# State-space matrices of a Hymba block on one core: turned by VectorE instead of TensorE, and the kernel blocks made in one visit

## The chip, the cores and the metric

The kernel runs on one core of one Trainium2 chip. The metric is the device time of one execution in microseconds, the median of three runs. The engines are TensorE (PE), VectorE (DVE), ScalarE (ACT), GpSimd (POOL) and SyncE (SP), which here only issues DMAs. Each engine runs its own instructions in order and waits on semaphores for the others.

## The reference

One block over x of 1 x 1024 x 1024 (1024 positions, width 1024), float32:

```
x = x + 1/2 * SwiGLU_1(RMSNorm(x))                 # 1024 -> 2816 -> 1024
h = RMSNorm(x); [q | k | v | u] = h @ w_in
attn = banded_sink_attention(q, k, v, sink)         # window 2 chunks of 64
ssm  = s5_ssm_glu(u, ...)
x = x + concat(RMSNorm(attn), RMSNorm(ssm)) @ w_out
x = x + 1/2 * SwiGLU_2(RMSNorm(x));  return RMSNorm(x)
```

The change lies in the state-space part: 32 groups g of 16 channels h, with 64 complex states p each:

```
lam_bar = exp(lam * exp(log_dt));  b_bar = ((lam_bar - 1) / lam) * b
s_t = lam_bar * s_(t-1) + b_bar u_t                 # associative scan over 1024 positions
y   = Re(c s) + d_skip * u;  z = gelu(y);  ssm = z * sigmoid(z @ w_glu + b_glu)
```

## The kernel before

**Products.** Every large product is made of fp32r parts: each factor is split into a high and a low part, and `mm3` (L1185 to L1187) issues three 128x128x512 matmuls, high by low, low by high and high by high. ACT makes the high parts (L1800, L1884), DVE the low ones (L2405, L2570, L2575).

**Order of the whole.** The first SwiGLU comes first, as 22 instances of seven products each (Strassen's scheme on gate and up, instances n = 0 to 21, `instance(n)` on each engine, 19.0 us each), then the down projection in 77 steps q (`down`, 12 matmuls, 2.72 us each). Then RMSNorm, the input projection, the mixer (state space and attention), the output projection, and the second SwiGLU like the first. In `down`, DVE works up to four steps ahead of PE: at step q it makes the parts of step q + 4 (`down_w`, `down_b`), and it adds weights (L2596) and takes results.

**State-space matrices.** They depend only on parameters, and POOL makes them beside the first SwiGLU, in one long chain of small operations in which each waits for the one before:
- It loads a_re, a_im and log_dt into `par` (`params`; L3107 issues log_dt, paced by the count of products that PE has done, `products(n, s)`), waits for them, and loads b (L3113, `load_b`) and c (L3118, `load_c`) at places of its chain where it works out the powers `lam` of lam_bar and `Bb`, that is b_bar.
- c comes as (g h) x p and is needed as p x (g h). PE transposes it at instance 10 (`c_tiles`, eight transposes), and ACT copies it to `CT` (`c_out`). POOL makes `CL`, c times the powers, from it.
- In a loop of four passes (from L3330, i = 0 to 3; four of the sixteen pairs j of groups each) POOL makes `EBb`, b_bar times the powers, to be E once turned, stores it to `eb_scratch` (L3356), waits for the store, since it writes the same buffer again (L3359), and makes and stores `cs`, the powers of the eighth power.
- Behind the loop, POOL adds squares for the sum of squares of the mixer's norm (L3071). They are issued in order, so they can't start before the loop has ended. PE reads the sum in `norm_sum` (L1211).

**Visits.** During the input projection PE leaves its large products for short visits. `WITH_PE` names them: at (unit, half) it lists the steps, each issued behind that unit's product. `WITH_ACT` and `MIXER_DVE` are ACT's and DVE's own lists. The steps are:
- E0 to E7 (`transposes_e`, L1485): four transposes each of `ebs`, which SP loaded from `eb_scratch`. ACT copies the results to `Et` (`e_out`). Two visits of four steps.
- K0 to K3 (`blocks_k`, L1479): the blocks of the convolution kernel, `Bb` times `CL`, 16 written matmuls of 64x16 by 64x128 a step, into partitions 0 to 15 of two banks. For g2 = 0 and 1 they use partitions 0 to 63 and 64 to 127 as input rows. ACT (`k_out`) and DVE (`k_first`, which adds d_skip on the diagonal, `dgl`) copy them to `kst`, and SP stores them to `k_scratch`. One visit each.
- I0 to I3 (`inject`, L1505): `Et` times `u8`, what u puts into the states. DVE takes it and scans.
- Y0 to Y3 (`outputs_y`, L1527, L1534): `Mt` times u8 plus `CL` times the states. `Mt` is read back from `k_scratch` (`load_m`).

Steps use banks 4 to 7 in turn (`ROUND`, `round_free`), so each waits for what was read four rounds before.

**SP's queue.** SP issues all of these loads and stores in one order, written out by hand (L1101 to L1145): behind the last product of the down projection x is stored and `ebs` and `CL` are loaded, then `load_in` (weights of the input projection), `store_u` and `load_u8` (u through memory into `u8`, L1046), `load_csn` (the powers cs), `store_k`, `load_m`, the bias, `store_y`. An issue of SP that waits holds back all that stand behind it.

Of the kernel before, what the change touches and what calls it, by code (L numbers as in the profile page):

```python
# [122 lines left out]
def taken_in(o):  # L123
# [30 lines left out]

ROUND = [((kind, 2 * b + i) if kind == "K" else (kind, b), 0 if kind == "K" else i)
         for kind, b in sum((WITH_PE[o] for o in sorted(WITH_PE)), []) if kind in "KEIY"
         for i in range(1 if kind == "E" else 2)]
# [242 lines left out]
CONST_DMAS = 4 + 2 + 1 + 8 + 1  # L400
# [23 lines left out]
def block_kernel(nc, x, ff1_norm, ff1_w_gate, ff1_w_up, ff1_w_down, mix_norm, w_in, sink, a_re, a_im,  # L424
# [85 lines left out]
    ebs = at("ebs", 64 * KB, [P, 2, NJ, P])  # L510
    csn = [at(f"csn{b}", (64 + 4 * b) * KB, [P, 2, 4, NC]) for b in range(4)]
# [3 lines left out]
    kst = [at(f"kst{i}", (80 + 4 * i) * KB, [GH, 8, P]) for i in range(2)]  # L515
# [3 lines left out]
    Et = at("Et", 162 * KB, [P, NJ, 2, P])  # L519
    Mt = at("Mt", 162 * KB, [P, NG, P])  # L520
    qT = at("qT", 162 * KB, [P, L // CHUNK, GQ, CHUNK])
    dgl = at("dgl", 178 * KB, [GH, NG, GH])
# [26 lines left out]
    dsk = small("dsk", [GH, NG])  # L549
# [99 lines left out]
    eb_d = nc.dram_tensor("eb_scratch", (P, 2, NJ, P), F32, kind="Internal").ap()  # L649
# [72 lines left out]
    ct_ready = sem("ct_ready")  # L722
# [2769 lines left out]
```

## Time and profile before

| | us |
|---|---|
| median of three runs | 1590.37 (1590.2 to 1590.79) |
| the profiled execution's own time | 1590.72 |
| its span | 1588.9 |
| PE busy | 1580.6 (99%) |
| DVE busy | 1096.8 (69%) |
| ACT busy | 714.3 (45%) |
| POOL busy | 512.5 (32%) |

The span is the time from the first to the last recorded instruction; the profiled execution took 1590.72 - 1588.9 = 1.8 us more, around it. Matmuls are pipelined: a record shows about 0.39 us for a large one, while the next starts 0.227 us behind it, so what PE spends is read from start to start. Busy time alone says little about the engines beside PE; what counts is whether PE has to wait for them.

### The profile page before, as it was taken

The numbers are of one execution on the slowest core, as the hardware profiler recorded it, in microseconds if no ns is written. First come the engines' busy times: TensorE is split into PE (matmuls) and PEld (weight loads), VectorE is DVE, ScalarE is ACT, GpSimd is POOL, SyncE is SP. The second block draws the span as 40 slices with busy tenths as digits, with TensorE's granted clock in tenths as the row PEclk, the third lists the DMA queues.
The fourth block names the chain that finished last, engine by engine and source line by source line (L and its number), as shares of the span: only waits on it lengthen the run. The fifth ranks groups of instructions, "written<-read, shape, count | busy, mean of one in ns | idle before, by whom it ended". The sixth has DMA issues, their size and how long they took to land.

```text
span 1588.9 us, 22029 instructions
## 1 busy us (share of the span) xinstructions
PE 1580.6 (99%) x7537; PEld 1305.3 (82%) x7537; DVE 1096.8 (69%) x1731; ACT 714.3 (45%) x1323; POOL 512.5 (32%) x938
## 2 busy tenths in 40 slices
PE   9999999999999999999999999999999999999998
PEld 7888888888888888888887888888888888888887
DVE  7966667766569886854369768766566666578766
ACT  7544343433334444532567544434344343344444
POOL 3005788877768778323030250000000000000000
PEclk9999999999999999999999999999999999999999
DMA  8253334433488545766631131433333333885443
GB/s 287 92 80 111 119 119 148 146 138 124 166 318 265 139 137 135 271 182 151 133 133 41 54 134 53 131 106 106 106 107 106 106 106 129 309 279 152 123 110 139
DMA packets 158455, 230.06 MB, mean 145 GB/s; under 512 B 25864, under 2 KB 95120, under 8 KB 154768
## 3 DMA queue, kind: packets, MB, share of 16 engines
q1 hardware_dynamic: 155120, 221.02, 43.6%
q0 software_dynamic: 3072, 7.62, 2.6%
q8 instruction: 61, 1.00, 0.3%
q14 instruction: 42, 0.34, 0.1%
q10 hardware_dynamic: 160, 0.07, 0.0%
HBM read 153.47 MB, written 74.15 MB: 143 GB/s over the span
## 4 chain that ended last, share of the span: by engine, by line
PE 98%; POOL 1%; ACT 0%; DMA 0%; DVE 0%; issue 0%; SPq 0%; DVEq 0%; POOLq 0%; ACTq 0%
PE bank L1185 31%; PE bank L1186 31%; PE bank L1187 31%; POOL ssq L3071 1%; PE bank L1552 1%; PE bank L1579 1%; PE bank L1534 0%; PE bank L1505 0%; PE bank L1479 0%; PE bank L1565 0%; PE bank L1527 0%; DMA x_in<-in_x_dram 0%; PE bank L1714 0%; PE bank L1219 0%; PE bank L1412 0%
## 5 line engine op out<-in xcount | busy, mean ns | idle before, releaser
L1185 PE MATMUL bank<-hbhi,ws_lo 128*128 128x512 f32 x1040 | 405.2, 390 | 0.0
L1187 PE MATMUL bank<-hbhi,ws_hi 128*128 128x512 f32 x1040 | 404.7, 389 | 0.0
L1186 PE MATMUL bank<-hblo,ws_hi 128*128 128x512 f32 x1040 | 404.6, 389 | 0.0
L1187 PEld LDWEIGHTS bank<-hbhi,ws_hi 128*128 128x128 f32 x1040 | 195.2, 188 | 40.7
L1185 PEld LDWEIGHTS bank<-hbhi,ws_lo 128*128 128x128 f32 x1040 | 195.2, 188 | 40.6 <-issue 0.4
L1186 PEld LDWEIGHTS bank<-hblo,ws_hi 128*128 128x128 f32 x1040 | 195.3, 188 | 40.3
L3071 POOL TENSOR_TENSOR ssq<-ssq,sqt 128x512 f32<-128x512 f32 x18 | 25.2, 1401 | 615.1 <-ACT sqt L1767 613.4
L1185 PE MATMUL bank<-d_hi,ws_lo 128*128 128x512 f32 x572 | 222.8, 389 | 0.0
L1187 PE MATMUL bank<-d_hi,ws_hi 128*128 128x512 f32 x572 | 222.5, 389 | 0.0
L1186 PE MATMUL bank<-d_lo,ws_hi 128*128 128x512 f32 x572 | 222.5, 389 | 0.0
L1837 ACT ACTIVATE loc<-bank 128x512 f32<-128x512 f32 x160 | 95.6, 597 | 251.6 <-PE bank L1187 251.6
L1884 ACT ACTIVATE d_hi<-d_in 128x512 fp32r<-128x512 f32 x154 | 96.0, 628 | 199.9 <-DMA d_in<-b_scratch 199.6
L2405 DVE TENSOR_TENSOR ws_lo<-w_sum,ws_hi 128x512 fp32r<-128x512 f32 x160 | 115.1, 719 | 97.3 <-ACT ws_hi L1800 97.3
L2575 DVE TENSOR_TENSOR d_lo<-d_in,d_hi 128x512 fp32r<-128x512 f32 x154 | 113.7, 740 | 82.9 <-ACT d_hi L1884 82.7
L1800 ACT ACTIVATE ws_hi<-w_sum 128x512 fp32r<-128x512 f32 x160 | 100.2, 626 | 76.2 <-PE bank L1187 60.1
L1185 PEld LDWEIGHTS bank<-d_hi,ws_lo 128*128 128x128 f32 x572 | 107.4, 188 | 22.7 <-issue 0.4
L1187 PEld LDWEIGHTS bank<-d_hi,ws_hi 128*128 128x128 f32 x572 | 107.4, 188 | 22.4
L1186 PEld LDWEIGHTS bank<-d_lo,ws_hi 128*128 128x128 f32 x572 | 107.4, 188 | 21.9
L1185 PE MATMUL bank<-hT_hi,w_lo 128*128 128x512 f32 x288 | 116.0, 403 | 0.0
L1186 PE MATMUL bank<-hT_lo,w_hi 128*128 128x512 f32 x288 | 112.4, 390 | 0.0
L1187 PE MATMUL bank<-hT_hi,w_hi 128*128 128x512 f32 x288 | 112.4, 390 | 0.0
L2405 DVE TENSOR_TENSOR ws_lo<-raw2a,ws_hi 128x512 fp32r<-128x512 f32 x78 | 55.0, 712 | 64.5 <-ACT ws_hi L1800 63.7
(319 smaller groups left out, 2696.6 us busy)
## 6 DMA issues: line engine op xcount, KB each, us to landing
b_scratch<-loc SPq DMA_DIRECT2D x42, 1024.0 KB, 7.3
d_in<-b_scratch SPq DMA_DIRECT2D x154, 256.0 KB, 3.1
raw2a<-in_ff_w_up_dram SPq DMA_DIRECT2D x42, 512.0 KB, 4.9
loc<-in_ff_w_gate_dram SPq DMA_DIRECT2D x36, 512.0 KB, 4.9
xT<-x_scratch SPq DMA_DIRECT2D x12, 1024.0 KB, 6.6
x_scratch<-xT SPq DMA_DIRECT2D x5, 2048.0 KB, 8.2
dw_lo_place<-in_ff_w_down_dram SPq DMA_DIRECT2D x8, 1024.0 KB, 7.9
x_in<-in_x_dram SPq DMA_DIRECT2D x8, 512.0 KB, 7.7
```

The source lines that it names most:

```text
L1185: nc.tensor.matmul(o, wl, rh, start=first, stop=False, skip_group_check=chain)
L1186: nc.tensor.matmul(o, wh, rl, start=False, stop=False, skip_group_check=chain)
L1187: return nc.tensor.matmul(o, wh, rh, start=False, stop=last, skip_group_check=chain)
L1552: last = nc.tensor.matmul(o, qT[r, n, 2 * a:2 * a + 2, :].rearrange("p g q -> p (g q)"), kTp[r, n * CHUNK:n * CHUNK + P], start=True, stop ...
L1579: last = nc.tensor.matmul(bank[V_BANK[m]][kv * HD:(kv + 1) * HD, nn * 256:(nn + 1) * 256], vwin[:, 2 * m + nn, kv * HD:(kv + 1) * HD], pts ...
L1800: act.activation(as_block(ws_hi[b][:, :]), weights(n, s), ACT.Copy).then_inc(ws_hi_done, 1)
L1837: act.activation(snap[w][:, i, :], bank[inst_bank(n, role)][:, :], ACT.Copy).then_inc(snap_taken, 1)
L1884: act.activation(d_hi[q % N_SLOT][:, :], d_in[q % N_SLOT][:, :], ACT.Copy).then_inc(d_hi_done, 1)
L2405: dve.tensor_tensor(as_block(ws_lo[b][:, :]), weights(n, s), as_block(ws_hi[b][:, :].bitcast(F32)), ALU.subtract).then_inc(ws_lo_done, 1)
L2575: dve.tensor_tensor(d_lo[q % N_SLOT][:, :], d_in[q % N_SLOT][:, :], d_hi[q % N_SLOT][:, :].bitcast(F32), ALU.subtract).then_inc(d_lo_done, 1)
L3071: pool.tensor_tensor(ssq_of(norm, h), ssq_of(norm, h), sqt_of(norm, a), ALU.add).then_inc(ssq_done, 1)
```

## The change

- `c_tiles` and `c_out` are gone. c is loaded in 16 pieces, laid out so that a transpose within blocks of 32 x 32 gives `CT`, and DVE does this in `turn_c` (two instructions) at instance 8. The loads move ahead in POOL's chain.
- `transposes_e`, `e_out` and `ebs` are gone. In each pass of POOL's loop DVE turns `EBb` to `EBt` (`turn_e`, two instructions, in blocks of 32 x 32), at instances 16 and 20 and at steps 21 and 52 of the down projection. POOL waits for the turn and stores `EBt` with four DMAs, in pieces of 128 bytes, into `et_scratch`; SP loads `Et` from there with four DMAs. POOL no longer waits for the store itself within a pass.
- `blocks_k` is one visit of 64 written matmuls behind unit 6, half 0. Its outputs lie at partitions 0, 32, 64 and 96 of two banks. `k_out` and `k_first` are two each instead of eight, the diagonal is laid out for 128 partitions, and `store_k` issues four DMAs for each of two g2; `load_m` waits for all eight.
- I3 comes behind Y0 in the same visit, at (10, 0) instead of (9, 1).
- a_re, a_im and log_dt are issued at earlier products: log_dt's last at the fourth product of instance 3 instead of instance 4. d_skip is loaded with eight DMAs instead of one.
- On SP's queue csn(0) and csn(1) come before load_in(4), and store_k(1) stands beside store_k(0).
- Buffers move: `Et`, `Mt` and the four `csn` change places, and POOL's loop has a temporary of its own.

The diff, cut to its core (removed lines are left out where the function stands above as it was):

```diff
-WITH_PE = {(1, 1): steps("m1"), (4, 0): steps("E0 E1 E2 E3"), (5, 0): steps("E4 E5 E6 E7"), (6, 0): steps("K0"), (6, 1): steps("I0"),
-           (7, 0): steps("I1 K1"), (7, 1): steps("I2"), (8, 0): steps("K2"), (8, 1): steps("K3"), (9, 1): steps("I3"),
-           (10, 0): steps("Y0"), (10, 1): steps("Y1"), (11, 1): steps("Y2"), (12, 0): steps("Y3")}
-
-WITH_ACT = {3: steps("e0 e1 e2 e3 W3"), 4: steps("e4 e5 e6 e7 W4"), 5: steps("k0 k1 W5"), 6: steps("k2 k3"),
-            7: steps("W6 k4 k5 k6 k7"), 9: steps("y0 W7"), 10: steps("y1"), 11: steps("y2 W8"),
+WITH_PE = {(1, 1): steps("m1"), (6, 0): steps("K0"), (6, 1): steps("I0"),
+           (7, 0): steps("I1"), (7, 1): steps("I2"),
+           (10, 0): steps("Y0 I3"), (10, 1): steps("Y1"), (11, 1): steps("Y2"), (12, 0): steps("Y3")}
+
+WITH_ACT = {3: steps("W3"), 4: steps("W4"), 5: steps("k0 k1 W5"),
+            7: steps("W6"), 9: steps("y0 W7"), 10: steps("y1"), 11: steps("y2 W8"),
             12: steps("y3 g0 g1"), 13: steps("W9 g2"), 14: steps("g3"), 15: steps("W10")}
-MIXER_DVE = steps("W3 D0 W4 d0 d1 W5 R0 R1 d2 d3 R2 W6 d4 d5 d6 d7 R3 b3 W7 v0 v1 W8 z0 z1 W9 z2 z3 W10")
+MIXER_DVE = steps("W3 D0 W4 d0 d1 W5 R0 R1 R2 W6 R3 b3 W7 v0 v1 W8 z0 z1 W9 z2 z3 W10")
...
+E_TURN_INST = {16: (0, 0), 20: (1, 2)}
+E_TURN_STEP = {21: 2, 52: 3}
+E_STORES = 4 + 1
+
+
...
-CONST_DMAS = 4 + 2 + 1 + 8 + 1
+CONST_DMAS = 4 + 2 + 1 + 8 + 8
 def src_of(tile, permuted):
...
-    ebs = at("ebs", 64 * KB, [P, 2, NJ, P])
-    kst = [at(f"kst{i}", (80 + 4 * i) * KB, [GH, 8, P]) for i in range(2)]
+    kst = at("kst", 80 * KB, [P, 2, 4, P])
-    Et = at("Et", 162 * KB, [P, NJ, 2, P])
+    Et = at("Et", 64 * KB, [P, NJ, 2, P])
+    EBt = at("EBt", a_v + 6 * KB, [P, 4, 2, P])
-    eb_d = nc.dram_tensor("eb_scratch", (P, 2, NJ, P), F32, kind="Internal").ap()
+    et_d = nc.dram_tensor("et_scratch", (32, NJ, 2, 4, P), F32, kind="Internal").ap()
...
         def load_csn(b):
-            sp.wait_ge(e_ready, 4 if b == 0 else 8)
             if b:
                 sp.wait_ge(cs_loaded, 16 * b)
+            if b == 2:
+                wait_lo(sp, 2 * KD)
             sp.dma_start(csn[b][:, :, :, :], cs_d[:, :, 4 * b:4 * b + 4, :]).then_inc(cs_loaded, 16)
         k_v = k_d.rearrange("g h c -> h g c")
-        def store_k(p):
-            sp.wait_ge(k_taken, 2 * p + 2)
-            if p:
-                sp.wait_ge(k_stored, 16 * p)
-            sp.dma_start(k_v[:, 8 * p:8 * p + 8, (T - 1) * GH:], kst[p % 2][:, :, :]).then_inc(k_stored, 16)
+        def store_k(g2):
+            sp.wait_ge(k_taken, g2 + 1)
+            for jj in range(4):
+                sp.dma_start(k_v[:, 2 * jj + g2::8, (T - 1) * GH:], kst[32 * jj:32 * jj + GH, g2, :, :]
+                             ).then_inc(k_stored, 16)
         def load_m(b):
             if b == 0:
                 sp.wait_ge(zero_stored, 48)
             if b >= 2:
                 sp.wait_ge(m_loaded[b % 2], 16 * T)
-            sp.wait_ge(k_stored, 16 * (b + 1))
+            sp.wait_ge(k_stored, 16 * 8)
...
-        sp.wait_ge(eb_stored, 4 * 32 + 16)
-        sp.dma_start(ebs[:, :, :, :], eb_d).then_inc(eb_loaded, 16)
+        sp.wait_ge(eb_stored, 4 * E_STORES * 16 + 16)
+        for b in range(P // 32):
+            sp.dma_start(Et[32 * b:32 * b + 32, :, :, :], et_d[:, :, :, b, :]).then_inc(et_loaded, 16)
         for i in range(2):
             sp.wait_ge(cl_stored[i], 16 * (NJ // 2))
         sp.dma_start(CL[:, :, :, :], cl_d).then_inc(cl_loaded, 16)
         load_in(3)
         sp.wait_ge(down_taken, 32)
         sp.dma_start(xs_d[:, 0:4, hs(1)], xT[:, 0:4, hs(1)]).then_inc(x_parked, 16)
+        load_csn(0)
+        load_csn(1)
         load_in(4)
         store_u(0)
-        load_csn(0)
         load_u8(0)
         load_in(5)
         store_u(1)
-        load_csn(1)
         load_u8(1)
         store_u(2)
         load_csn(2)
         load_u8(2)
         load_csn(3)
         store_k(0)
+        store_k(1)
         load_in(6)
         load_m(0)
-        store_k(1)
         store_u(3)
         load_in(7)
         load_u8(3)
         load_m(1)
-        store_k(2)
         load_m(2)
         load_glu(0)
-        store_k(3)
-        sp.wait_ge(k_stored, 64)
         sp.dma_start(biast[:, :, :], bias_c).then_inc(bias_loaded, 16)
         load_m(3)
...
+        def blocks_k(_):
+
+            pe.wait_ge(cl_loaded, 16)
             for g2 in range(2):
...
+                round_free("K", g2)
+            for p in range(4):
                 for ri in range(2):
...
+                    for jj in range(4):
+                        for g2 in range(2):
+                            r = slice(g2 * NS, (g2 + 1) * NS)
+                            last = nc.tensor.matmul(bank[round_bank("K", g2)][32 * jj:32 * jj + GH, p * P:(p + 1) * P],
+                                                    Bb[r, ri, 4 * p + jj, :], CL[r, ri, 4 * p + jj, 0:P],
+                                                    start=ri == 0, stop=ri == 1, skip_group_check=True)
+                            if p == jj == 3 and ri:
+                                last.then_inc(k_ready, 1)
         def inject(b):
-            pe.wait_ge(e_taken, 2 * b + 2)
+            pe.wait_ge(et_loaded, 64)
...
+        def k_out(g2):
+
+            act.wait_ge(k_ready, g2 + 1)
+            src = bank[round_bank("K", g2)][:, :].rearrange("q (p m) -> q p m", p=4)[:, :, GH:]
+            act.activation(kst[:, g2, :, GH:], src, ACT.Copy).then_inc(k_act, 1)
...
             for q in range(6 * N_PAIR):
                 p, j = divmod(q, N_PAIR)
+                if q in E_TURN_STEP and w == 0:
+                    turn_e(E_TURN_STEP[q])
...
+            if E_TURN_INST.get(n, (0, 1))[1] == 0:
+                turn_e(E_TURN_INST[n][0])
             ahead_sum(0)
             ahead(0)
             ahead_sum(1)
             ahead(1)
             ahead_sum(2)
             ahead(2)
+            if E_TURN_INST.get(n, (0, 0))[1]:
+                turn_e(E_TURN_INST[n][0])
             gate_c12(n)
...
+        def turn_e(b):
+
+            dve.wait_ge(eb_made, b + 1)
+            for ri in range(2):
+                dve.transpose(EBt[:, :, ri, :], EBb[:, ri, :, :]).then_inc(eb_turned, 1)
+
...
+        def turn_c():
+
+            dve.wait_ge(c_loaded, 16 * 16)
+            for ri in range(2):
+                dve.transpose(CT[:, ri, :, :].rearrange("p j h -> p (j h)"),
+                              c_in[:, ri, :, :].rearrange("p j s -> p (j s)")).then_inc(ct_taken, 1)
...
         def diagonal(_):
             wait_lo(dve, 2 * KD)
-            dve.tensor_tensor(dgl[:, :, :], ident[0:GH, 0:GH].unsqueeze(1).to_broadcast([GH, NG, GH]),
-                              dsk[:, :].unsqueeze(2).to_broadcast([GH, NG, GH]), ALU.mult).then_inc(diag_chain, 1)
-
...
+            dve.tensor_reduce(dmask[:, :], ident[:, :].rearrange("q (j m) -> q m j", j=4)[:, 0:GH, :], AX.X, ALU.add
+                              ).then_inc(diag_chain, 1)
             dve.wait_ge(diag_chain, 1)
...
+            dve.tensor_tensor(dgl[:, :, :], dmask[:, :].unsqueeze(1).to_broadcast([P, 8, GH]),
+                              dsk[:, :].unsqueeze(2).to_broadcast([P, 8, GH]), ALU.mult).then_inc(diag_chain, 1)
+
+        def k_first(g2):
+
+            dve.wait_ge(diag_chain, 2)
+            dve.wait_ge(k_ready, g2 + 1)
+            dve.wait_ge(k_act, g2 + 1)
+            src = bank[round_bank("K", g2)][:, :].rearrange("q (p m) -> q p m", p=4)[:, :, 0:GH]
+            dve.tensor_tensor(kst[:, g2, :, 0:GH], src, dgl[:, 4 * g2:4 * g2 + 4, :], ALU.add).then_inc(k_taken, 1)
...
-            pool.dma_start(dsk[:, :], d_skip[0].rearrange("(g h) -> h g", h=GH)).then_inc(consts_loaded, 16)
+            for jj in range(4):
+                for g2 in range(2):
+                    pool.dma_start(dsk[32 * jj:32 * jj + GH, 4 * g2:4 * g2 + 4],
+                                   d_skip[0].rearrange("(p j g h) -> j g h p", p=4, j=4, g=2)[jj, g2]).then_inc(consts_loaded, 16)
             for n, a in enumerate((a_re, a_im)):
                 for g2 in range(2):
-                    pool.wait_ge(product_done, products(2 + n, 3 * g2))
+                    pool.wait_ge(product_done, products(2, 4 * n + 2 * g2))
                     pool.dma_start(par[g2 * NS:(g2 + 1) * NS, n, :],
                                    a[0].rearrange("(j g) p -> g p j", g=2)[g2]).then_inc(params_loaded, 16)
             for g2 in range(2):
-                pool.wait_ge(product_done, products(4, 3 * g2))
+                pool.wait_ge(product_done, products(3, 1 + 2 * g2))
                 pool.dma_start(par[g2 * NS:(g2 + 1) * NS, 2, :],
...
+        def load_c(n, g2):
+
+            for sh in range(2):
+                for jj in range(2):
+                    q = 64 * g2 + 32 * sh + GH * jj
+                    pool.dma_start(c_in[q:q + GH, n, :, :],
+                                   (c_re, c_im)[n][0].rearrange("(j a g) h s -> a g h j s", a=2, g=2)[jj, g2][:, :, 32 * sh:32 * sh + 32]
+                                   ).then_inc(c_loaded, 16)
...
+        load_c(0, 0)
+        load_c(0, 1)
         exp_parts(xr)
+        load_c(1, 0)
+        load_c(1, 1)
...
-            if k % 2:
-                load_c(k // 4, k // 2 % 2)
...
-                pool.tensor_tensor(mark[:, :], unit[:, 0, 0, :], unit[:, 0, 0, :], ALU.mult)
-
-            pool.wait_ge(eb_stored, i * 32 + 16)
+                return pool.tensor_tensor(mark[:, :], unit[:, 0, 0, :], unit[:, 0, 0, :], ALU.mult)
+
+            pool.wait_ge(eb_stored, i * (E_STORES * 16) + 16)
             for ri in range(2):
...
-            passed()
-            pool.dma_start(eb_d[:, :, bass.ds(i * 4, 4), :], EBb[:, :, :, :]).then_inc(eb_stored, 16)
-            pool.wait_ge(eb_stored, i * 32 + 32)
+            passed().then_inc(eb_made, 1)
+            pool.wait_ge(eb_turned, i * 2 + 2)
+            for a in range(P // 32):
+                pool.dma_start(et_d[:, bass.ds(i * 4, 4), :, :, 32 * a:32 * a + 32].rearrange("c j r b s -> c (j r b) s"),
+                               EBt[32 * a:32 * a + 32, :, :, :].rearrange("c j r (b s) -> c (j r b) s", s=32)
+                               ).then_inc(eb_stored, 16)
...
```

## Rows read from the trace of the kernel before

**Rows 1.** The page: its first line, and the shares by engine of part 4.
```profile
span 1588.9 us, 22029 instructions
...
PE 98%; POOL 1%; ACT 0%; DMA 0%; DVE 0%; issue 0%; SPq 0%; DVEq 0%; POOLq 0%; ACTq 0%
```

**Rows 2.** Timeline of PE around the c transposes: start us, us, engine, line, operation.
```profile
214.14 0.39 PE L1187 MATMUL bank<-hbhi,ws_hi 128*128 128x512 f32 x1
...
215.70 0.40 PE L1187 MATMUL bank<-hbhi,ws_hi 128*128 128x512 f32 x1
```

**Rows 3.** The same around the first of two visits of E transposes.
```profile
676.97 0.39 PE L1187 MATMUL bank<-hT_hi,w_hi 128*128 128x512 f32 x1
...
679.41 0.40 PE L1187 MATMUL bank<-hT_hi,w_hi 128*128 128x512 f32 x1
```

**Rows 4.** The same around the first of four K visits.
```profile
691.41 0.39 PE L1187 MATMUL bank<-hT_hi,w_hi 128*128 128x512 f32 x1
...
694.17 0.40 PE L1187 MATMUL bank<-hT_hi,w_hi 128*128 128x512 f32 x1
```

**Rows 5.** The same around the visit of the fourth injection.
```profile
725.03 0.39 PE L1187 MATMUL bank<-hT_hi,w_hi 128*128 128x512 f32 x1
...
727.82 0.39 PE L1187 MATMUL bank<-hT_hi,w_hi 128*128 128x512 f32 x1
```

**Rows 6.** Chain of waits, four of the visits of PE: start us, us, what.
```profile
691.80 1.85 PE bank L1479 x32
...
708.86 1.90 PE bank L1505 x32
...
725.41 1.90 PE bank L1505 x32
...
730.26 1.78 PE bank L1527 x16
```

**Rows 7.** POOL timeline: the last log_dt load, and the work behind it.
```profile
111.47 0.82 POOL L3107 DMA_DIRECT2D par<-in_log_dt_dram  x1 [7.34 <-PE bank L1187]
...
130.81 0.82 POOL L3113 DMA_DIRECT2D b_raw<-in_b_re_dram  x1 [18.52 <-DMA par<-in_log_dt_dram]
```

**Rows 8.** Line that stores E: ns min/median/max, first and last start us.
```profile
L3356 POOLq MOVE eb_scratch<-EBb x4: 29/38/38, 340.8 to 585.5; - x4
L3356 POOL DMA_DIRECT2D eb_scratch<-EBb x4: 679/679/682, 341.4 to 586.1; - x4
```

**Rows 9.** POOL timeline: behind stores three and four, and the sums of squares.
```profile
503.16 0.84 POOL L3359 TENSOR_TENSOR EBb<-unit 128x8 f32<-128x8 f32 x1 [3.25 <-DMA eb_scratch<-EBb]
...
590.32 0.69 POOL L3359 TENSOR_TENSOR EBb<-unit 128x8 f32<-128x8 f32 x1 [3.54 <-DMA eb_scratch<-EBb]
...
626.76 8.18 POOL L3071 TENSOR_TENSOR dw_hi_place<-dw_hi_place 128x512 f32<-128x512 f32 x5
```

**Rows 10.** Timeline of PE: the product that reads the sum of squares.
```profile
634.46 0.60 PE L1211 MATMUL bank<-ident,dw_hi_place 128*128 128x128 f32 x4
```

**Rows 11.** Timeline of DVE at the four places where a turn is put.
```profile
331.06 0.81 DVE L2387 TENSOR_TENSOR w_sum<-raw2a 128x512 f32<-128x512 f32 x1
...
415.20 0.69 DVE L2405 TENSOR_TENSOR ws_lo<-w_sum,ws_hi 128x512 fp32r<-128x512 f32 x1 [1.32 <-ACT ws_hi L1800]
...
502.05 0.68 DVE L2570 TENSOR_TENSOR ws_lo<-dw_lo_place,ws_hi 128x512 fp32r<-128x512 f32 x1
...
585.15 0.81 DVE L2570 TENSOR_TENSOR ws_lo<-dw_a,ws_hi 128x512 fp32r<-128x512 f32 x1
```

**Rows 12.** The line with DVE's transposes of v: columns as in Rows 8.
```profile
L2799 DVE STREAM_TRANSPOSE vTp<-bank x2: 717/718/718, 743.8 to 753.2; 128x512 f32<-128x512 f32 x2
```

**Rows 13.** Timeline of the DMA issues of SP: the third load of u8.
```profile
698.87 3.62 SPq L1046 DMA_DIRECT2D u<-u_scratch  x8
```

**Rows 14.** The same line's landing times.
```profile
DMA to landing us min/median/max: 2.2/2.8/3.3
```

**Rows 15.** DMA issues by line: form, count, KB each, median us to landing.
```profile
ebs<-eb_scratch SPq DMA_DIRECT2D x1, 2048.0 KB, 7.9
```

More of the change, by code:

```diff
@@ L152 @@
 STATE_STEPS = 4 * 5 + 8
+E_TURN_INST = {16: (0, 0), 20: (1, 2)}
+E_TURN_STEP = {21: 2, 52: 3}
+E_STORES = 4 + 1
 ROUND = [((kind, 2 * b + i) if kind == "K" else (kind, b), 0 if kind == "K" else i)
-         for kind, b in sum((WITH_PE[o] for o in sorted(WITH_PE)), []) if kind in "KEIY"
-         for i in range(1 if kind == "E" else 2)]
+         for kind, b in sum((WITH_PE[o] for o in sorted(WITH_PE)), []) if kind in "KIY"
+         for i in range(2)]
 def round_number(kind, b, i=0):
@@ L509, in block_kernel @@
     zT_lo = at("zT_lo", 48 * KB, [P, 4, L], F32R)
-    ebs = at("ebs", 64 * KB, [P, 2, NJ, P])
-    csn = [at(f"csn{b}", (64 + 4 * b) * KB, [P, 2, 4, NC]) for b in range(4)]
+    csn = [at(f"csn{b}", (162 + 4 * b) * KB, [P, 2, 4, NC]) for b in range(4)]
     yT = at("yT", 64 * KB, [P, 4, L])
@@ L548, in block_kernel @@
     dec8 = small("dec8", [P, NJ])
-    dsk = small("dsk", [GH, NG])
+    dsk = small("dsk", [P, 8])
     zero = small("zero", [P, (T - 1) * GH])
@@ L1379, in x_tiles @@
                     last.then_inc(xt_done, 1)
-        def c_tiles():
-            pe.wait_ge(c_loaded, 64)
-            for ri in range(2):
-                for i in range(4):
-                    last = nc.tensor.transpose(bank[6 + ri][:, i * P:(i + 1) * P],
-                                               c_in[:, ri, i, :, :].rearrange("p a s -> p (a s)"), ident[:, :])
-                last.then_inc(ct_ready, 1)
         def first_half(norm):
@@ L1467, in round_free @@
                 pe.wait_ge(y_taken, 2 * b + i + 1)
-        def blocks_k(p):
-            if p == 0:
-                pe.wait_ge(cl_loaded, 16)
+        def blocks_k(_):
+            pe.wait_ge(cl_loaded, 16)
             for g2 in range(2):
-                round_free("K", 2 * p + g2)
-            for jj in range(4):
+                round_free("K", g2)
+            for p in range(4):
                 for ri in range(2):
-                    for g2 in range(2):
-                        r = slice(g2 * NS, (g2 + 1) * NS)
-                        last = nc.tensor.matmul(bank[round_bank("K", 2 * p + g2)][0:GH, jj * P:(jj + 1) * P],
-                                                Bb[r, ri, 4 * p + jj, :], CL[r, ri, 4 * p + jj, 0:P],
-                                                start=ri == 0, stop=ri == 1)
-                        if jj == 3 and ri:
-                            last.then_inc(k_ready, 1)
-        def transposes_e(b):
-            pe.wait_ge(eb_loaded, 16)
-            round_free("E", b)
-            for jj in range(2):
-                for ri in range(2):
-                    m = 2 * jj + ri
-                    last = nc.tensor.transpose(bank[round_bank("E", b)][:, m * P:(m + 1) * P],
-                                               ebs[:, ri, 2 * b + jj, :], ident[:, :])
-            last.then_inc(e_ready, 1)
+                    for jj in range(4):
[6 more added lines that the diff above has]
+                                last.then_inc(k_ready, 1)
         def inject(b):
-            pe.wait_ge(e_taken, 2 * b + 2)
+            pe.wait_ge(et_loaded, 64)
             pe.wait_ge(u8_loaded, 16 * T * (b + 1))
@@ L3347, in _ @@
                 ilink(pool.tensor_copy(cR[:, ri], rot8[:, ri, bass.ds(i * 4, 4)]))
-            q = [ptmp[:, n, 0:4 * GH].rearrange("p (j h) -> p j h", h=GH) for n in range(2)]
+            q = [ptmp_e[:, n, 0:4 * GH].rearrange("p (j h) -> p j h", h=GH) for n in range(2)]
             for t in range(T):
@@ L3361, in _ @@
             while n < NC:
-                v = [ptmp[:, m, 0:4 * n].rearrange("p (j c) -> p j c", j=4) for m in range(2)]
+                v = [ptmp_e[:, m, 0:4 * n].rearrange("p (j c) -> p j c", j=4) for m in range(2)]
                 w = [cR[:, m, :].unsqueeze(2).to_broadcast([P, 4, n]) for m in range(2)]
```

75 lines of the change are left out of this document (20 added, 55 removed).

## The prediction

> **What bounds the kernel now.** I read the shares by engine of the chain of waits first: 98% of a span of 1588.9 us lies on PE [rows 1]. So a product taken from PE moves the end by its own length, and work of any other engine costs nothing until PE waits for it. Then I read PE's timeline around the visits that the change touches, to price a visit from the spacing of the large products on both sides: undisturbed, one follows the next at 0.227 us, so three intervals are 0.68. Last come the timelines of POOL, DVE and the DMA queue of SP. There one is to see how long before PE needs it each thing is ready, since nearly everything that the change takes from PE goes to them. The profiled execution took 1590.72 us, 1.8 of it outside the span, and lies 0.35 over the median of 1590.37. I subtract from 1590.72 and give the median's number at the end.
>
> **What PE loses.** The c transposes: 215.70 - 214.14 = 1.56 for three intervals and eight transposes, 0.88 more than 0.68 [rows 2]. The E transposes: 679.41 - 676.97 - 0.68 = 1.76 a visit, two visits, 3.52 [rows 3]. The kernel blocks: 694.17 - 691.41 - 0.68 = 2.08 a visit, four visits, 8.32 [rows 4]. Of each, 1.85 is its 32 matmuls (the code writes 16; a float32 one is recorded as two) [rows 6]. Two of them can run side by side (g2 = 0 and 1 sit on different rows of the array): 16 rounds of 0.116. The other 0.23 is going in and out. Now there is one visit of 128 recorded matmuls whose outputs start at partitions 0, 32, 64 and 96. If all eight that an inner loop (jj, g2) writes run side by side, there are again 16 rounds: 2.1. If only pairs do, there are 64: 7.4 + 0.2 = 7.6. No row shows four column places at once. I take 2.1, because the rows show two places going at the cost of one with nothing to spare paid for it, both for rows (these) and for columns (the injections, 128*64, 32 in 1.90 [rows 6]). The gain is 6.2, and 0.7 at the other end.
>
> The fourth injection costs 727.82 - 725.03 - 0.68 = 2.11 [rows 5] and 1.90 of that is its matmuls. Put behind Y0 it keeps these and saves one way in and out, less the switch from Y0's form: 0 to 0.2, I take 0.1. PE's sum is 0.9 + 3.5 + 6.2 + 0.1 = 10.7.
>
> Against the 2.1 speaks the spacing: in a visit of now one matmul starts per 58 ns (1.85 / 32) [rows 6], and 128 in 1.9 would be one per 15, which no row shows. The Trainium skill, TensorE: Matmul & The Clock Gate, section "Wait — 56ns, not 53.3ns?", says that starts do not come closer than about 25 ns on average, however small the matmuls are; by that, as an estimate, the visit is 3.4 and the gain 1.3 less. No run here decides it, since 58 ns is above that floor.
>
> **What DVE gains: the turns.** Eight transposes of 128x512 in four turns and two of 128x256 for c. A 128x512 transpose takes 0.72 [rows 12], a turn 1.4, all ten 6.5 us. DVE is not on the chain; what counts is where it has to wait for POOL, and when POOL goes on. Diagonal and K sums shrink from nine small instructions to four: nothing.
>
> POOL's chain starts earlier. It waited for the second log_dt load, issued at 111.47 and used at 130.81 [rows 7]; that issue now waits for the fourth product of instance 3 instead of 4, one instance or 19.0 us before. Against that come 16 issues for c where there were four. At 0.82 an issue [rows 7] 12 more are 9.8. So the first E is ready 9.2 before 340.8 [rows 8], at 331.6. The turn stands in DVE's order at 331.06 [rows 11], 0.9 less with PE ahead: a wait of 1.4 and a turn of 1.4, in a stretch where DVE stands idle between splits anyway (1.32 before one of them [rows 11]). The c turn comes at the start of instance 8: five instances behind the issue of log_dt, which is 19.0 before 111.47 [rows 7], so near 178. POOL goes on at 111.8 and issues all of c some 40 us later at most. Neither turn costs.
>
> The E batches are (585.5 - 340.8) / 3 = 81.6 apart [rows 8], so the second is ready near 413, before its turn at 415.20 less 0.9 plus one split [rows 11]. The third, near 415.5 + 81.6 + 0.7 = 498, is before its turn at 502.05 [rows 11]: here POOL waits for DVE, 4 us. Behind the turn it issues four stores of 128-byte pieces where it had one and waited for it: 4 x 0.82 + 1.4 = 4.7 after the turn begins. It goes on at 506.8, where it went on at 503.16 [rows 9]. From there to the fourth E were 585.5 - 503.16 = 82.3: ready at 589.1, and DVE, there at 585.15 [rows 11], waits about 4. DVE works up to four steps of 2.72 (12 matmuls of 0.227) ahead of PE, 10.9, and has two splits of 0.8 to do for that step: PE does not feel a wait of 4. But POOL goes on at 589.1 + 4.7 = 593.8 for 590.32 [rows 9], and with it its adds for the sum of squares begin at about 630.2 instead of 626.76. Five take 8.18 [rows 9], the four that the sum needs 6.5: ready at 636.8. PE wants them at 634.46 [rows 10], less 0.9 for c: 633.6. That is a stall of 3.2. While DVE stands still POOL runs free of it and gets some back: I take 3.0. Bounds: 0, if the chain of 82.3 shrinks by 3.4, and 5, if the strided stores cost 1.0 to issue each and adds do not quicken.
>
> **What moves on SP's queue.** E's load goes straight to Et, 2 MB in 512-byte pieces for 16 KB ones (7.9 to land [rows 15]), in front of CL and w_in, and csn 0 and 1 come before load_in(4). store_u, the loads of u8, and load_m stand behind these. What is late is seen at the third injection. Its u8 was issued from 698.87 to 702.49 [rows 13], and landed 2.8 after the last issue at 702.1 [rows 14]: 704.9, for a visit at 708.86 [rows 6], 4.0 before. PE is now there 0.9 + 3.5 + 2.1 = 6.5 earlier (the second K visit lay between). The queue is earlier by 0.9 with PE and by 0.6 for a csn issue taken out, but the first loads wait behind more bytes. So PE waits 6.5 - 4.0 - 1.0 = 1.5 there. Behind it come eight stores of K where there was one by then, two times 4 loads of 0.45, then load_m(0) and u8's last load, which lands about when PE, at 730.26 - 10.6 + 1.5 = 721.2 [rows 6] plus 3.8 for Y0, reaches the fourth injection. That is what its place behind Y0 is worth: in its old place it would have been 4 us short. Bounds of this term: 0 and 4.
>
> **Sum.** 10.7 - 3.0 - 1.5 = 6.2: 1584.5 against the profiled execution, 1584.2 as a median.
>
> **Rivals.** (a) The covers hold: POOL is quicker with DVE's pauses, u8 lands in time, and PE keeps 9 to 10.7 of its gain: 1580.6. For it: no visit in rows 2 to 5 has a gap before it that its matmuls don't explain. Against it: the arithmetic of rows 9 to 11, which leaves POOL 1 us of room.
> (b) The change does not do what it says for K: the eight matmuls do not run side by side, and the visit takes 7.6 as four visits' rounds did. The gain is 5.2, less the 3.0 of POOL; PE then comes later to the injections and that stall falls away: 2.2, 1588.2. By the Trainium skill's floor on matmul starts, cited above, the time would be an estimated 1585.5, between the two.
> (c) Slower: POOL's stores. An issue of 1024 pieces of 128 bytes with a stride may cost POOL far more than the 0.82 of a 1024-piece load [rows 7]. Only the eight issues of turns three and four count, since POOL waits for DVE before them. PE's stall is 3.2 plus eight times the excess; it eats the 9.2 (10.7 less 1.5) when an issue costs 1.6 and goes beyond "same" at 2.0. At 2.6 it is 3.0 + 14.2 against 9.2: 8 slower, 1598.4. Against it: POOL's present store of E, 1024 pieces with a stride, takes 0.68 [rows 8].
>
> **Chances.** About 0.2% (3.2 us) is what a measurement tells from no change. The forecast, with its two stalls at 2 to 6 together, 0.5; (a) 0.24; (b) 0.14; (c) 0.04; stalls beyond 6 us in all, 0.08. Faster: the forecast and (a) nearly whole, a third of (b): 0.80. Same: the rest of (b) and most of the last, 0.15. Slower: 0.05. The range takes in (a) with 10.7, 1579.7, and (b), 1588.4.
>
> **What would show it.** The K visit near 2.1 in PE's timeline; no transposes of c or E there; PE's matmul on the sum of squares behind a gap of about 3, with POOL's adds beginning near 630; DVE waiting about 4 before the fourth turn; a gap of 1 to 2 before the third injection, none before Y0 to Y3. PE's work before and behind is untouched. A K visit over 4, POOL's adds at 627 or before, or a stretch of DVE transposes over 1 us each would make it wrong.

## The result: slower, and the profile after

The changed kernel takes 1595.11 us (median of 12 runs, 1591.03 to 1597.57) for 1590.47: a ratio of 1.0028 (95% interval 1.0019 to 1.0036), 4.6 us slower, small but beyond the 3.2 us that the prediction set for telling a change. The forecast was 1584.2, with 5 in 100 for slower. The twelve times of the changed kernel lie 6.5 us apart, those of the kernel before 0.6; the profile shows one execution (1594.48 us).

The page of the changed kernel, first line and shares of the chain of waits, beside [rows 1]:

```profile
span 1592.8 us, 21976 instructions
...
PE 89%; POOL 6%; issue 2%; DMA 1%; POOLq 0%; DVE 0%; ACT 0%; SPq 0%; DVEq 0%; ACTq 0%
```

PE's share of the chain fell from 98% to 89%: it now waits for others, and the view of PE's waits says where (us in total, times, longest):

```profile
PE bank L1216 <- POOL dw_hi_place L3050: 5.1, 1, 5.1
PE bank L1486 <- issue: 4.6, 1, 4.6
```

"issue" here is a wait whose last release the profile doesn't name. By the queue of SP below it is u8: its eight loads are issued until 707.14, and PE goes on at 709.10. PE's timeline at the two places and at the K visit (start us, us, engine, line, operation), beside [rows 10], [rows 4] and the injections of [rows 6]:

```profile
633.03 0.39 PE L1192 MATMUL bank<-d_hi,ws_hi 128*128 128x512 f32 x1
638.52 1.11 PE L1216 MATMUL bank<-ident,dw_hi_place 128*128 128x128 f32 x4 [5.10 <-POOL dw_hi_place L3050]
639.28 0.78 PE L1190 MATMUL bank<-d_hi,ws_lo 128*128 128x512 f32 x1
639.86 0.63 PE L1191 MATMUL bank<-d_lo,ws_hi 128*128 128x512 f32 x1
...
694.14 0.39 PE L1192 MATMUL bank<-hT_hi,w_hi 128*128 128x512 f32 x1
694.46 2.00 PE L1471 MATMUL bank<-CL,Bb 64*16 64x128 f32 x128
...
696.96 0.40 PE L1192 MATMUL bank<-hT_hi,w_hi 128*128 128x512 f32 x1
...
704.08 0.39 PE L1192 MATMUL bank<-hT_hi,w_hi 128*128 128x512 f32 x1
709.10 3.68 PE L1486 MATMUL bank<-u,Et 128*64 128x128 f32 x32 [4.63 <-issue]
712.71 0.80 PE L1190 MATMUL bank<-hT_hi,w_lo 128*128 128x512 f32 x1
713.30 0.63 PE L1191 MATMUL bank<-hT_lo,w_hi 128*128 128x512 f32 x1
713.73 0.63 PE L1192 MATMUL bank<-hT_hi,w_hi 128*128 128x512 f32 x1
```

Read the starts. Behind either gap the large matmuls stand 0.43 us apart and not 0.227, and the injection takes 3.61 (712.71 - 709.10) for 1.90. Windows of the same stretches and of undisturbed ones follow (us, busy and count of PE, PEld, DVE, ACT and POOL, then the granted clock, the DMA share and GB/s):

```profile
620.00:633.00 13.00, 13.00 (x59) 10.78 (x58) 7.10 (x11) 4.22 (x7) 10.83 (x25) 1.00 0.69 182
638.50:643.00 4.50, 4.48 (x13) 3.71 (x14) 3.81 (x7) 3.31 (x8) 3.09 (x3) 0.50 0.01 2
643.50:660.00 16.50, 16.50 (x76) 13.67 (x75) 15.43 (x24) 9.76 (x17) 6.18 (x5) 1.00 0.72 239
709.10:714.50 5.40, 5.40 (x36) 4.77 (x37) 3.43 (x9) 0.00 (x0) 3.41 (x3) 0.50 0.60 185
```

The granted clock is 0.50 behind each gap, 1.2 GHz for 2.4. A gap is paid twice.

Where the 3.9 us between the two spans come from, read from start to start of the same matmuls in the two traces:

| what | us |
|---|---|
| up to the sum of squares: the c transposes, and 0.3 of small shifts | -1.2 |
| the E transposes | -3.6 |
| four K visits for one | -6.0 |
| the fourth injection behind Y0 | -0.2 |
| a short wait near 921, gone | -0.3 |
| gap before the sum of squares | +5.3 |
| gap before the second injection, and 0.2 before the first | +4.9 |
| low clock behind the first gap, behind the second | +2.2, +2.8 |

Together 3.9. SP's queue shows the second gap's origin (start us, us from the first issue of a group to its last, count):

```profile
668.75 2.27 SPq L1120 DMA_DIRECT2D x_scratch<-xT  x1
671.08 14.03 SPq L1059 DMA_DIRECT2D csn<-cs_scratch  x2
685.15 0.60 SPq L852 DMA_DIRECT2D raw<-in_w_in_dram  x1
685.80 0.57 SPq L1042 DMA_DIRECT2D u_scratch<-ust  x1
692.98 3.64 SPq L1052 DMA_DIRECT2D u<-u_scratch  x8
...
697.14 1.32 SPq L1042 DMA_DIRECT2D u_scratch<-ust  x1
703.51 3.63 SPq L1052 DMA_DIRECT2D u<-u_scratch  x8
```

The same loads in the kernel before:

```profile
679.14 0.63 SPq L1052 DMA_DIRECT2D csn<-cs_scratch  x1
681.12 4.14 SPq L1046 DMA_DIRECT2D u<-u_scratch  x8
...
686.47 0.58 SPq L1052 DMA_DIRECT2D csn<-cs_scratch  x1
691.29 4.50 SPq L1046 DMA_DIRECT2D u<-u_scratch  x8
```

`load_csn(1)` waits for the landing of csn(0). That was issued behind the store of x and the loads of Et and CL and took 13.4 us to land (the longest of the four csn loads), so the queue stands 14 us between the two. The first u8 load begins at 692.98 where it began at 681.12, the second at 703.51 for 691.29. And POOL, in its fourth pass (the turn that it waited for, its four stores, the next step):

```profile
588.94 1.62 POOL L3347 DMA_DIRECT2D et_scratch<-EBt  x2 [2.04 <-DVE EBt L2662]
594.36 1.56 POOL L3347 DMA_DIRECT2D et_scratch<-EBt  x2 [3.81 <-issue]
595.94 3.15 POOL L3351 TENSOR_TENSOR EBb<-unit 128x8 f32<-128x8 f32 x1
...
632.64 1.32 POOL L3050 TENSOR_TENSOR dw_hi_place<-dw_hi_place 128x512 f32<-128x512 f32 x1
```

Two stores, a pause of 3.8, two stores, then a small operation that takes 3.15 where it took 0.69 [rows 9]. The adds begin at 632.64 for 626.76 [rows 9].

### The profile page after: what moved, and what is told of

The parts are those of the page before. It is cut to its first block, busy times and chain, and to the rows that moved or that the text cites. A ratio compares the mean times of both kernels' runs of the same rounds, so it can differ in the third digit from the quotient of the medians.

```text
span 1592.8 us, 21976 instructions
## 1 busy us (share of the span) xinstructions
PE 1574.9 (99%) x7497; PEld 1301.0 (82%) x7497; DVE 1099.9 (69%) x1736; ACT 706.8 (44%) x1305; POOL 527.2 (33%) x970
## 4 chain that ended last, share of the span: by engine, by line
PE 89%; POOL 6%; issue 2%; DMA 1%; POOLq 0%; DVE 0%; ACT 0%; SPq 0%; DVEq 0%; ACTq 0%
PE bank L1190 28%; PE bank L1191 28%; PE bank L1192 28%; POOL ptmp_e L3358 1%; POOL EBb L3360 1%; POOL ptmp_e L3359 1%; PE bank L1486 1%; PE bank L1533 1%; POOL ptmp_e L3341 1%; POOL EBb L3343 1%; POOL ptmp_e L3342 1%; PE bank L1560 1%; PE bank L1515 0%; PE bank L1546 0%; PE bank L1508 0%
```

## Experiments

Ratios are to the kernel before, on the same chip.

**e1: csn back in its place.**

```diff
-        load_csn(0)
-        load_csn(1)
         load_in(4)
         store_u(0)
+        load_csn(0)
         load_u8(0)
         load_in(5)
         store_u(1)
+        load_csn(1)
         load_u8(1)
```

> The changed kernel with load_csn(0) back behind store_u(0) and load_csn(1) back behind store_u(1) on SP's queue. Theory A (csn(1) waits on the queue for csn(0), 14 us from 671.1 to 685.1, so that u8 of the second injection is issued 12 us later than before and PE stands 4.6 us, then runs at half clock for some us): that gap and the slow stretch behind it go, together about 7 us, 1588 by the median 1595.1; a gap of 0 to 2 may show at the third injection. Rival B (the load of Et in 512-byte pieces fills the DMA queue and delays u8, whatever the order): the gap before the second injection stays within 1.5 of 4.6 and the time is within 2 us of the changed kernel's 1595.1.

1589.62 us, 0.9991 (0.9982 to 1.0000); 5.5 under the changed kernel for 7 expected. The gap at the second injection is gone, with its low clock, and one of 1.5 stands before the third:

```profile
711.16 1.97 PE L1486 MATMUL bank<-u,Et 128*64 128x128 f32 x32 [1.54 <-issue]
```

The prediction had 1.5 there, for its own order of the queue. The gap before the sum of squares is still there, 4.1. Rival B falls: Et is loaded in the same four pieces ahead of everything else, and the second injection doesn't wait.

**e2: DVE's turns earlier.**

```diff
-E_TURN_INST = {16: (0, 0), 20: (1, 2)}
-E_TURN_STEP = {21: 2, 52: 3}
+E_TURN_INST = {16: (0, 0), 20: (1, 0)}
+E_TURN_STEP = {19: 2, 51: 3}
```

> The changed kernel with DVE's turns earlier: the second at the start of instance 20, the third at step 19, the fourth at step 51. Theory A (POOL's chain is late because it stands 7.3, 4.9 us and 2.0 for turns that DVE has not come to; its adds then hold PE for 5.1 us, with a stretch of half clock behind): the adds begin near 627 instead of 632.6, the gap of 5.1 before PE's sum of squares falls under 1 and the clock stays up there: 7 us less, 1588. Rival B (DVE, which now waits for POOL at the turns, hands the wait on to PE's weights, or POOL's stores are what costs): PE gets new gaps of 1 to 3 us near 408, 497 or 582, or the adds still begin behind 630, and the time is within 3 us of 1595.1.

1587.28 us, 0.9980 (0.9970 to 0.9989). POOL's timeline:

```profile
626.06 8.15 POOL L3050 TENSOR_TENSOR dw_hi_place<-dw_hi_place 128x512 f32<-128x512 f32 x5
```

PE no longer waits for the sum of squares and has no new wait for weights. The gap at the second injection is still there, 4.9, and the injection behind it takes 3.6 for 1.9. So each of the two stalls alone was enough to eat most of the gain.

**e3: both.**

> Both edits, csn back and turns early. Theory A: no gap of PE over 1 us in 630 to 760 beside one of 0 to 2 at the third injection, clock at full level: 1590.4 less 10.7 of PE's work plus 0 to 2, so 1580 to 1582. Rival B (the changed kernel's time is lost in something else, such as slower large matmuls beside more small packets): over 1585.

1582.13 us, 0.9945 (0.9932 to 0.9959). The only gap of PE over 1 us in 600 to 760 is before the third injection:

```profile
701.81 0.39 PE L1192 MATMUL bank<-hT_hi,w_hi 128*128 128x512 f32 x1
704.25 2.89 PE L1486 MATMUL bank<-u,Et 128*64 128x128 f32 x32 [2.05 <-issue]
707.07 0.79 PE L1190 MATMUL bank<-hT_hi,w_lo 128*128 128x512 f32 x1
```

Here even 2.05 us brought a slow stretch (the injection took 2.82 from start to start, for 1.90). It doesn't come in every execution of e3: the profiled one took 1583.09 us at a mean granted clock of 0.998, the fastest 1580.83 at 1.0.

**e4, e5, e12: a gap and nothing else.** The kernel before, with n small products of 128x1 on POOL ahead of its adds, each waiting for the last.

```diff
+        for i in range(n):
+            pool.tensor_tensor(ptmp[:, 0, 0:1], unit[:, 0, 0, :], unit[:, 0, 0, :], ALU.mult).then_inc(pool_chain, 1)
+            pool.wait_ge(pool_chain, base_links + 4 * LINKS_PER_BATCH + i + 1)
         norm(N_MIX)
```

> The kernel before, with 20 small additions of POOL put ahead of its adds for the sum of squares, so that PE stands about 5 us there and nothing else is changed. Theory A (a gap of about 5 us lowers PE's clock to half for some us behind it, which costs 2 to 2.5 more): 1590.4 + 5 + 2.3 = about 1597.5, with large matmuls 0.43 apart behind the gap. Rival B (the low clock in the changed kernel comes from something else; the gap costs its length alone): 1595.4 and large matmuls 0.227 apart behind it.

> The kernel before with 35 small additions of POOL ahead of its adds (20 gave a gap of 0.9 us), each 0.29 us, so about 4.3 us more: a gap of PE near 5 us. Theory A (a gap of 5 us brings half clock behind it): large matmuls 0.43 us apart for about 4 us, time 1590.6 + 5.1 + 2.4 = 1598. Rival B (the low clock belongs to the changed kernel's work, not to the gap): 0.227 apart, 1595.7.

> The kernel before with 28 small additions of POOL ahead of its adds, between the 20 and 35 of e4 and e5 (gaps of 0.9 and 5.0 us): a gap of about 3 us. Theory A (the clock falls behind a gap only from some length on): either the time is 1590.4 + 3.0 - and large matmuls stand 0.227 apart behind it, 1593.4, or the clock falls and it is 1595 to 1596. Rival B (the price grows in step with the gap, 6.5 us for 5.0): 1594.3 with part of the stretch slow.

With n = 20 the gap came out at 0.9 us, and not the 5 that I wanted: 1591.45 us, 1.0008 (0.9999 to 1.0017), clock unchanged in the profiled execution. Two of the ten runs took 1594.0 and 1594.8 at a mean clock of 0.998, where the others have 0.999 to 1.0. The gap was small because POOL came out of its loop earlier: its first added product begins at 623.25, where the adds of the kernel before began at 626.76 [rows 9], with nothing changed ahead of it. e5 (623.07) and e12 (622.33) show the same. So the time at which POOL ends this chain differs by 3.5 to 4.4 us between traces of the same work. With n = 35 the gap was 5.0:

```profile
633.84 0.39 PE L1187 MATMUL bank<-d_hi,ws_hi 128*128 128x512 f32 x1
639.25 0.90 PE L1211 MATMUL bank<-ident,dw_hi_place 128*128 128x128 f32 x4 [5.02 <-POOL dw_hi_place L3071]
639.79 0.78 PE L1185 MATMUL bank<-d_hi,ws_lo 128*128 128x512 f32 x1
640.37 0.63 PE L1186 MATMUL bank<-d_lo,ws_hi 128*128 128x512 f32 x1
```

1596.93 us, 1.0035 (1.0022 to 1.0049): 6.5 us for a gap of 5.0, in a kernel whose work is that of before. The granted clock is 0.54 from 639.3 to 643.0, with nothing but the gap changed: the low clock belongs to the gap, and rival B of both runs falls. With n = 28 the profiled execution had a gap of 2.4 and no slow stretch, while its runs spread from 1590.19 to 1596.78 (median 1594.5, 1.0021, 1.0011 to 1.0031). The profile shows one of these only, so the price of a gap of that size isn't settled by it.

**e6: e3 with the third store of u earlier,** on a semaphore of its own.

```diff
         store_u(1)
         load_csn(1)
-        load_u8(1)
         store_u(2)
-        load_csn(2)
+        load_u8(1)
         load_u8(2)
+        load_csn(2)
         load_csn(3)
```

> As e3, and the third store of u is issued before the second load of u8, on a semaphore of its own, and csn(2) behind the third load. Theory A (the third injection waits 2.0 us for u8, whose issue at 697.67 waits for the landing of the store issued at 694.31): u8(2) is issued about 1 us earlier (it still waits for the landing of the second load), the gap shrinks from 2.0 to about 1, and the time is 1 to 2.5 under e3, 1580 to 1581. Rival B (the issue is bound by the landing of the second load alone): no change of the gap beyond 0.3.

The gap at the third injection went from 2.05 to 1.06, as expected. But the time rose to 1585.67 us, 0.9967 (0.9955 to 0.9979), 3.5 over e3: I had put csn(2) and csn(3) behind each other, and SP's queue shows the same fault as in the change, at a smaller size:

```profile
690.31 11.53 SPq L1053 DMA_DIRECT2D u<-u_scratch  x16
701.95 4.62 SPq L1060 DMA_DIRECT2D csn<-cs_scratch  x2
706.61 3.89 SPq L1067 DMA_DIRECT2D k_scratch<-kst  x8
```

u8's last load came late and PE stood 4.0 before the fourth injection, which then took 3.6 for 1.9.

**e9: e6 with csn(2) between the loads.**

```diff
         load_u8(1)
+        load_csn(2)
         load_u8(2)
-        load_csn(2)
         load_csn(3)
```

> As e6, with csn(2) between the second and the third load of u8, so that csn(3) no longer stands right behind it on SP's queue. Theory A (in e6, as in the changed kernel, one csn load right behind another makes the queue stand for the landing of the first, there 4 us, and everything behind is late, u8's last load above all): the gap of 4.0 at the fourth injection goes, the one at the third stays near 1.0, and the time is 1.5 to 2.5 under e3, near 1580. Rival B (the early third store itself delays what stands behind it): a gap over 2 stays at the fourth injection and the time is over 1583.

1580.88 us, 0.9939 (0.9926 to 0.9953): the fastest of the runs with more than one time, 9.5 us under the kernel before and 14.2 under the changed one. The gap of 4.0 is gone, 1.2 is left at the third injection and 0.3 at the second, and the clock stays up:

```profile
704.10 1.97 PE L1487 MATMUL bank<-u,Et 128*64 128x128 f32 x32 [1.23 <-issue]
```

 It differs from the changed kernel only in where three turns and three issues stand, and in one semaphore.

**e7: e3 with the fourth injection in its old place.**

```diff
-           (7, 0): steps("I1"), (7, 1): steps("I2"),
-           (10, 0): steps("Y0 I3"), ...
+           (7, 0): steps("I1"), (7, 1): steps("I2"), (9, 1): steps("I3"),
+           (10, 0): steps("Y0"), ...
```

> As e3, with the fourth injection back behind unit 9, before Y0. Theory A (its place behind Y0 hides u8's last load): PE gets there at about 718.1, u8 lands at about 722.5, a gap of about 4.4 us and perhaps a stretch of low clock: 1586.5 to 1588 for e3's 1582.1. Rival B (Y0 waits anyway, or the load comes sooner when asked for sooner): within 1 us of e3.

1588.93 us, 0.9991 (0.9982 to 1.0000), 6.8 over e3. PE waits 4.97 there, and the clock falls behind it:

```profile
716.35 0.39 PE L1192 MATMUL bank<-hT_hi,w_hi 128*128 128x512 f32 x1
721.71 3.68 PE L1486 MATMUL bank<-u,Et 128*64 128x128 f32 x32 [4.97 <-issue]
725.32 0.80 PE L1190 MATMUL bank<-hT_hi,w_lo 128*128 128x512 f32 x1
```

This edit, worth 0.2 by its own length, carries 6.8. The third injection waits 1.9 in this trace, and no slow stretch follows.

**e8: e3 with the K matmuls by column place.**

```diff
-            for p in range(4):
-                for ri in range(2):
-                    for jj in range(4):
+            for jj in range(4):
+                for p in range(4):
+                    for ri in range(2):
```

> As e3, with the 64 matmuls of the K visit ordered by column place first (jj outermost), so that only g2 = 0 and 1 alternate next to each other. Theory A (the visit takes 2.1 since eight neighbours in the order run side by side on different rows and columns of the array): 64 rounds of 0.116, the visit 7.4 to 7.6, the time 5 to 6 us over e3, 1587.5. Rival B (matmuls that small start as fast in any order): the visit stays at 2.1 and the time at 1582.

```profile
686.50 0.39 PE L1192 MATMUL bank<-hT_hi,w_hi 128*128 128x512 f32 x1
686.82 5.92 PE L1471 MATMUL bank<-CL,Bb 64*16 64x128 f32 x128
692.68 0.50 PE L1190 MATMUL bank<-hT_hi,w_lo 128*128 128x512 f32 x1
```

The same 128 recorded matmuls take 5.86 from start to start for 1.93 (694.46 to 696.39 in the changed kernel), by their order alone. Their single starts show why: in the changed kernel eight neighbours start within 0.05 us and the next eight 0.12 behind the first; here two start 0.007 apart and the next two 0.11 behind. Since a record's end is modelled, the overlap is read from the starts: eight neighbours in the order run side by side, and matmuls for the same place follow each other. A pair takes 0.092 on average (5.86 / 64) and not 0.116; where the column place changes, starts come closer. Yet the time is 1583.33 us, 0.9959 (0.9943 to 0.9974), only 1.2 over e3: u8 has landed by the time PE reaches the third injection, and its gap and slow stretch are gone.

**e10, e11: POOL's pause in the fourth pass.** It stands in the traces of the changed kernel and of all its variants between the same two stores, 2.9 to 3.8 us, also where the adds are no longer late. Both runs are e3 with one edit; e10 first:

```diff
-E_TURN_STEP = {19: 2, 51: 3}
+E_TURN_STEP = {19: 2, 57: 3}
```

> As e3, with the fourth turn at step 57 of the down projection, where DVE stands idle over 1 us between its splits, instead of step 51, where its instructions follow each other without a pause. A probe for the pause of 3.3 us that POOL makes between its second and third store of the fourth pass; PE will stand some 15 us for the adds, which is not the point. Theory A (DVE's instructions without a pause keep POOL from writing the stores' descriptors): the pause falls under 1 us. Rival B (the queue behind POOL's stores is full after so many descriptors, whatever DVE does): a pause of 3 to 4 us between the same two stores.

```profile
598.86 1.62 POOL L3347 DMA_DIRECT2D et_scratch<-EBt  x2 [17.66 <-DVE EBt L2662]
603.86 1.56 POOL L3347 DMA_DIRECT2D et_scratch<-EBt  x2 [3.39 <-issue]
```

The pause is 3.4 though DVE stands idle twice beside it, for 1.3 and 1.7 (600.2 to 601.5 and 602.8 to 604.5): a DVE that runs without a break is not what makes it. (1596.48 us, one run; PE stands 10.2 for the adds.) Then e11:

```diff
+        for a in range(4):
+            pool.dma_start(spare_d[a, :, :, 0, :],
+                           Bb[32 * a:32 * a + 32, :, :, :].rearrange("c r (x j) h -> c (r x) (j h)", j=2)
+                           ).then_inc(spare, 16)
+        pool.wait_ge(spare, 64)
         with pool.Fori(0, NJ // 4) as i:
```

> As e3, with four extra DMAs on POOL's queue ahead of its loop, together as many pieces of 128 bytes as two stores of EBt (from Bb to a spare place in memory). Theory B of e10, now the standing one (the pause of 3.3 us comes at a fixed count of what POOL has written into its DMA queue): the pause between the second and third store of the fourth pass goes, and one of about 3 us stands two stores earlier, ahead of the first store of that pass or inside the third pass. Rival (it belongs to the fourth pass itself, its place in the code or the load of the DMA engines there): the pause stays between the same two stores.

```profile
585.25 1.63 POOL L3354 DMA_DIRECT2D et_scratch<-EBt  x2 [3.34 <-DVE EBt L2664]
590.04 1.56 POOL L3354 DMA_DIRECT2D et_scratch<-EBt  x2 [3.16 <-issue]
```

The pause did not move, so it doesn't come at a fixed count of pieces written either; the theory that I called standing falls. (1580.84 us, one run.) It belongs to the fourth pass, and its cause stays open. What is shown is its size.

## Why the prediction was wrong, step by step

- **What PE loses**: 11.0 us (the first four rows of the table) for 10.7, right. The c and E transposes and the fourth injection measured as forecast. The K visit costs 2.14 (696.96 - 694.14 - 0.68) for 2.1. The four visits of before are worth 8.1 and not 8.3, since the second shared one way in and out with an injection. I had set 15 ns a record against the floor of about 25 ns that the Trainium skill gives (TensorE: Matmul & The Clock Gate, "Wait — 56ns, not 53.3ns?"): 128 records took 1.93, which on average is 15 ns for each record and 30 for each of the 64 matmuls written. Counted by record, as I had counted, the floor does not hold in this trace; only the average by written matmul lies above it.
- **DVE gains the turns**: no cost by themselves. A turn took 1.30 for 1.4, and DVE waited 1.25 before the first for 1.4 and 2.8 before the fourth for 4. POOL had the second E ready at 409.5 for the 413 forecast and stood 7.3 until it was turned, so the lead was lost; e2 gives it back. In no run did PE wait for weights because of a turn.
- **POOL's adds**: they were forecast to begin at 630.2 and a stall of 3.0; they began at 632.6 and PE stood 5.1. The steps hold up to the fourth turn (POOL went on at 506.98 for 506.8, E was ready at 586.7 for 589.1). What failed is "4.7 after the turn begins": four stores of 0.78 and no more. From the turn's beginning they took 9.0 (586.93 to 595.94) for 4.7, because of the pause of 3.8 and 0.7 between the turn's end and the first store. The small operation of 3.15 behind them did not decide it: in e1 it takes 0.22, and the adds begin at 632.31 all the same. The upper bound that I gave to this stall, 5, was passed by a little. And the base of this sum, adds at 626.76 in one trace, was less firm than I took it: e4, e5 and e12 show POOL 3.5 to 4.4 us earlier at that point with the same work.
- **What moves on SP's queue**: this step failed. I wrote that csn 0 and 1 come before load_in(4) and counted the bytes ahead of them, but not that csn(1) waits for csn(0)'s landing on an in-order queue: 14 us. I looked for the stall at the third injection and got 1.5, with bounds 0 and 4; it came at the second, 4.6. e1, where that wait is gone, shows 1.5 at the third, the number that I had worked out, and e3 2.05; that order of the queue is not the one I forecast for, so the agreement is in part luck. The line `sp.wait_ge(cs_loaded, 16 * b)` stood in the code; where it was before, the queue passed it at no cost (csn(1) is issued at 686.47, right behind its neighbour).
- **A gap costs its length**: never written down, and wrong. Both stalls took PE's clock to 0.50 behind them, 5.0 us in all, and e5 shows the same with no other change. Without that the kernel would have been 1.1 us faster than before by its span (3.9 - 5.0) and not slower. I had not weighed it, since PE has no gap in the middle of the kernel before that could show it. The Trainium skill (TensorE: Matmul & The Clock Gate, "HAM oscillation — how this bites in real kernels") describes a kernel whose TensorE waits for a DMA so long that it comes back throttled to half clock. The runs agree, with 1.6 to 2.8 us of extra time behind gaps of 4.0 to 5.3 (e1, e2, e5, e6, e7 and the changed kernel).
- **The fourth injection**: right in what its place is worth. I wrote that in its old place it would have been 4 us short; e7 shows 5.0, and 6.8 with the clock.
- **Rivals**: (b) did not come true, but e8 shows what it would have cost alone: 5.9 for the visit and little of it in the time. (c), the strided stores, was near in kind, since POOL's stores are where a good part of one stall arose; but an issue took 0.78, and what held them up was a single pause. "Stalls beyond 6 us in all" had 0.08 and held the truth: they were 5.1 and 4.6, and 5.0 of low clock came on top. The range was too narrow because every rival priced one stall at a time, and each at its bare length.

## What to carry to other kernels

When loads are moved on an in-order queue, write beside each issue what it waits for, and ask of each wait whether it is still satisfied at the new place; two loads of which the second waits for the first must not stand next to each other. Price a wait of a full-speed TensorE at more than its length once it reaches some us: here gaps of about 5 cost 6.5 to 7.5. And when PE's work shrinks, everything that feeds it comes due earlier by as much, so that a gain of 11 us only shows (e9) once the helpers are moved too.

## What the runs showed of the hardware

- PE comes back at half clock (1.2 GHz) from a gap: large matmuls or an injection at the slow spacing for 3.6 to 5.9 us behind gaps of 4.0 to 5.3 us. In the profiled executions there is none behind 0.9 to 1.5 (e4, e6, e9, e11, e1); a slow stretch behind 2.05 in e3 and 2.2 in e10, none behind 1.9 in e7 and 2.4 in e12. So length alone does not decide in this range.
- Matmuls of 64 rows by 16 columns at eight places of the array run side by side when they are neighbours in the order: 128 records in 1.93 us (changed kernel). With two places alternating they take 5.86 (e8).
- Small operations of POOL can go at DVE's pace: behind the third turn (507 to 514 in the changed kernel) they start 0.60 us apart, as DVE's own 128x512 TENSOR_TENSOR do, and 0.29 apart from 515.15 to 517.7 with DVE idle. It depends on what DVE runs: in e5 the 35 products of POOL start 0.29 apart on average (10.27 / 35), though DVE's SCALAR_TENSOR_TENSOR on a bank fill 622.3 to 627.2 without a break.
- The same chain of POOL, unchanged up to its end, came out of the loop 3.5 to 4.4 us apart (626.76 in the kernel before; 623.25, 623.07 and 622.33 in e4, e5 and e12).
